# A 16th up-projection pair by seven products in the first MLP, and two moved low parts in the last two

## The reference, cut to what matters

```python
h2 = rms_norm(x, ffn_norm)                       # first MLP
u = causal_dwconv(h2 @ w_up, conv_w, conv_b)
a, bval = jnp.split(u, 2, axis=-1)
x = x + (jax.nn.silu(a) * bval) @ w_down
...
hn = rms_norm_2(h, norm_mix_g[1]); qkv = hn @ w_qkv      # second layer, ahead of its attention
...
h = jax.nn.relu(xn @ w_in); y = (h * h) @ w_out          # last two MLPs
```

## Time and profile before

| | us |
|---|---|
| median of 3 runs | 1708.62 (1707.88 to 1710.52) |
| profiled execution | 1708.18 |
| its span | 1705.8 |
| PE busy | 1693.6 (99%) |
| DVE, ACT, POOL busy | 1135.9, 899.8, 1022.7 |

### The profile page before, as it was taken

The page is one execution under the profiler, slowest core; times in us unless marked ns, Lnnn a source line. Parts: engine busy times, 40 slices in busy tenths (PEclk is TensorE's granted clock), DMA queues, the critical chain, the costliest instruction groups (busy, mean ns, idle before and its releaser), DMA issues.

```text
span 1705.8 us, 28211 instructions
## 1 busy us (share of the span) xinstructions
PE 1693.6 (99%) x9965; PEld 1456.8 (85%) x9965; DVE 1135.9 (67%) x2214; ACT 899.8 (53%) x1635; POOL 1022.7 (60%) x1076
## 2 busy tenths in 40 slices
PE   9999999999999999999999999999999999999998
PEld 7778889999888778888989898977777889898988
DVE  6875788887411455667767666777777675757576
ACT  5665556787422444435454544556565454535355
POOL 6444678787654434457565657755554665666666
PEclk9999999999999999999999999999999999999999
DMA  5221332332223222223323232232321232222222
GB/s 190 78 69 53 109 116 95 116 108 83 92 99 142 96 69 84 73 84 116 109 89 112 87 112 90 94 129 84 117 105 52 87 136 99 99 100 99 100 98 75
DMA packets 48682, 168.17 MB, mean 99 GB/s; under 512 B 5376, under 2 KB 6672, under 8 KB 48528
## 3 DMA queue, kind: packets, MB, share of 16 engines
q1 hardware_dynamic: 48272, 166.05, 28.4%
q10 hardware_dynamic: 288, 0.52, 0.1%
HBM read 164.31 MB, written 2.24 MB: 98 GB/s over the span
## 4 chain that ended last, share of the span: by engine, by line
PE 88%; DVE 5%; POOL 3%; issue 2%; ACT 2%; DMA 1%; SPq 0%; DVEq 0%; ACTq 0%; POOLq 0%
PE bank L928 18%; PE bank L1690 6%; PE bank L1699 6%; PE bank L1691 6%; PE bank L852 6%; PE bank L853 6%; PE bank L858 6%; PE bank L1268 3%; PE bank L1276 3%; PE bank L1269 3%; PE bank L946 3%; PE bank L952 3%; PE bank L947 3%; PE bank L1329 2%; PE bank L1320 2%; PE bank L1322 2%
## 5 line engine op out<-in xcount | busy, mean ns | idle before, releaser
L624 POOL TENSOR_TENSOR w_lo<-stage,w_hi 128x256 fp32r<-128x256 f32 x664 | 527.2, 826 | 423.4 <-ACT w_hi L1752 220.7
L1752 ACT ACTIVATE w_hi<-stage 128x1024 fp32r<-128x1024 f32 x166 | 174.7, 1053 | 165.8 <-PE bank L928 51.8
L853 PE MATMUL bank<-xn_lo,w_hi 128*128 128x512 f32 x544 | 211.8, 389 | 0.0
L852 PE MATMUL bank<-xn_hi,w_hi 128*128 128x512 f32 x544 | 211.8, 389 | 0.0
L928 PE MATMUL bank<-xn_hi,w_hi 128*128 128x512 f32 x464 | 189.0, 407 | 0.0
L928 PE MATMUL bank<-xn_lo,w_hi 128*128 128x512 f32 x464 | 181.8, 392 | 0.0
L3424 DVE TENSOR_TENSOR x<-x,bank 128x256 f32<-128x256 f32 (+1 forms) x217 | 97.5, 455 | 89.2 <-PE bank L1699 86.5
L1699 PE MATMUL bank<-arena 128*128 128x256 f32 x896 | 146.6, 283 | 0.0
L858 PE MATMUL bank<-xn_hi,w_lo 128*128 128x512 f32 x544 | 135.0, 389 | 0.0
L1690 PE MATMUL bank<-arena 128*128 128x256 f32 x512 | 129.4, 284 | 1.2 <-DVE arena L3444 0.6
L1691 PE MATMUL bank<-arena 128*128 128x256 f32 x512 | 128.7, 283 | 0.0
(11 more groups left out here) (506 smaller groups left out, 4305.1 us busy)
## 6 DMA issues: line engine op xcount, KB each, us to landing
stage<-weights SPq DMA_DIRECT2D x189, 512.0 KB, 3.2
stage<-pairs SPq DMA_DIRECT2D x46, 512.0 KB, 3.3
prob<-pairs SPq DMA_DIRECT2D x32, 512.0 KB, 3.2
bias<-table SPq DMA_DIRECT2D x11, 896.0 KB, 5.4
xn_raw<-pairs SPq DMA_DIRECT2D x14, 512.0 KB, 4.2
out<-y SPq DMA_DIRECT2D x8, 256.0 KB, 2.2
x<-x_in SPq DMA_DIRECT2D x3, 512.0 KB, 7.4
bias<-swa_table SPq DMA_DIRECT2D x4, 256.0 KB, 3.5
```

The source lines that it names most:

```text
L624: ins = nc.gpsimd.tensor_tensor(w_lo[:, p_, ks], stage[:, p_, ks], w_hi[:, p_, ks].bitcast(F32), ALU.subtract)
L852: pe.matmul(G[p_][:], w_hi[:, p_, k], hi[:, k], start=(first and k == ks[0]), stop=False)
L853: mm = pe.matmul(G[p_][:], w_hi[:, p_, k], lo[:, k], start=False, stop=False)
L1752: act.activation(w_hi[:, p_], stage[:, p_], ACT.Copy).then_inc(hi_ready, 1)
```

## The change

The edits:

1. N_PLAIN 7 to 6, so Q_UP 16, N_UP1 12. FACTORS_AT stays, so factor quad 3 is made during the last pair but one. The 16th quad lies in `stage`; SP's wait ahead of the down tiles is for quad 15's A22 low part.
2. POOL's list: since 3 is now N_PLAIN - 3, the low parts of factor quads 2 and 3 both come behind the split of the last plain tile.
3. POOL makes T1's low part of factor quad 3 alone, then A11's low part of quad 0, then the low parts of T3, T2 and T4.
4. S1 of quad 0 waits for the first of these, S2 of quad 0 (and ACT's S4 high) for the last.
5. `tile(..., inside=4)`: the norm's two matmuls come after three of the eight weight blocks of tile 1.
6. In the last factor quad of each round of the last two MLPs, ACT and DVE make T2's high and low part first, DVE ahead of adding product S1, then T3's and T4's together.
7. The count of `factor_low` that S2's last block waits for goes with it.

```diff
-N_PLAIN = 7
+N_PLAIN = 6
...
+X_LOWS = QUADS + 1
...
+        outer_sums = flat_tmp[:, 5 * HS:8 * HS].rearrange("p (c s) -> p c s", c=3)[:, 0:3:2]
...
                 pool.wait_ge(ffh_ready, 2 * k + 2)
                 ks = slice(k * HS, (k + 1) * HS)
-                nc.gpsimd.tensor_tensor(factor[:, F_T1:, 1, ks], factor_parts[k % 2][:, 2 * S:].rearrange("p (c s) -> p c s", c=4),
-                                        factor[:, F_T1:, 0, ks].bitcast(F32), ALU.subtract).then_inc(factor_low, 1)
+                e = factor_parts[k % 2]
+                if k < QUADS - 1:
+                    nc.gpsimd.tensor_tensor(factor[:, F_T1:, 1, ks], e[:, 2 * S:].rearrange("p (c s) -> p c s", c=4),
+                                            factor[:, F_T1:, 0, ks].bitcast(F32), ALU.subtract).then_inc(factor_low, 1)
+                    return
+                nc.gpsimd.tensor_tensor(factor[:, F_T1, 1, ks], e[:, 2 * S:2 * S + HS], factor[:, F_T1, 0, ks].bitcast(F32),
+                                        ALU.subtract).then_inc(factor_low, 1)
+                if N_PLAIN - 2 in FACTORS_AT:
+                    up_low(HI_A11, 0)
+                nc.gpsimd.tensor_tensor(factor[:, F_T3:, 1, ks], e[:, 2 * S + HS:].rearrange("p (c s) -> p c s", c=3),
+                                        factor[:, F_T3:, 0, ks].bitcast(F32), ALU.subtract).then_inc(factor_low, 1)
...
-            for k in (HI_A11, HI_A12, HI_S4):
+            for k in (HI_A12, HI_S4) if N_PLAIN - 2 in FACTORS_AT else (HI_A11, HI_A12, HI_S4):
...
+                if inside is not None:
+                    highs(ks[:3], True)
+                    norm(inside)
+                    highs(ks[3:], False).then_inc(hi_free, 1)
+                    pe.wait_ge(lo_ready, 2 * m + p_ + 1)
+                    lows(ks, True).then_inc(tile_done, 1)
...
                 elif k == HI_S2:
                     pe.wait_ge(up_moved, moved_at(q, P1_COPY))
+                    if q == 0:
+                        pe.wait_ge(factor_low, X_LOWS)
...
-                norm(4)
-                tile(T // 2, 1, xn_hi, xn_lo)
+                tile(T // 2, 1, xn_hi, xn_lo, inside=4)
...
-                    if j == 0:
+                    if j == 0 and i == QUADS - 1 and f == F_T2:
+                        pe.wait_ge(factor_low, X_LOWS + N_CH * l + n + 1)
+                    elif j == 0:
...
-            act.wait_ge(factor_low, QUADS)
+            act.wait_ge(factor_low, X_LOWS)
...
+                            if i == QUADS - 1:
+                                act.wait_ge(u_ready, fc_at(l, n, i) + 3)
+                                act.activation(fc_hi[:, i, F_T2], flat_tmp[:, 6 * HS:7 * HS], ACT.Copy).then_inc(factor_made, 1)
+                                act.wait_ge(u_ready, fc_at(l, n, i) + 4)
+                                act.activation(fc_hi[:, i, F_T3:F_T4 + 1:2], outer_sums, ACT.Copy).then_inc(ffh_ready, 1)
...
                         if e == KD - 1:
+                            dve.wait_ge(factor_made, QUADS + N_CH * l + n + 1)
+                            dve.tensor_tensor(fc_lo[:, i, F_T2], flat_tmp[:, 6 * HS:7 * HS], fc_hi[:, i, F_T2].bitcast(F32),
+                                              ALU.subtract).then_inc(factor_low, 1)
                             add_product(q, HI_S1)
...
+                            dve.wait_ge(ffh_ready, FFH_BEFORE + u + 4)
+                            dve.tensor_tensor(fc_lo[:, i, F_T3:F_T4 + 1:2], outer_sums, fc_hi[:, i, F_T3:F_T4 + 1:2].bitcast(F32),
+                                              ALU.subtract).then_inc(ff_ready, 1)
```

More of the change, by code:

```diff
@@ L833, in _, with tile @@
             skip = [0]
-            def tile(m, p_, hi, lo, nk=KD, ready=None, late=None):
+            def tile(m, p_, hi, lo, nk=KD, ready=None, late=None, inside=None):
                 pe.wait_ge(hi_ready, 2 * m + p_ + 1)
@@ L859, in lows @@
                     return mm
-                if ready is None and late is None:
+                if inside is not None:
[4 more added lines that the diff above has]
+                    lows(ks, True).then_inc(tile_done, 1)
+                elif ready is None and late is None:
                     highs(ks, True).then_inc(hi_free, 1)
@@ L2457, in mlp2 @@
                                            ACT.Copy).then_inc(ffh_ready, 1)
-                            act.wait_ge(u_ready, fc_at(l, n, i) + 4)
-                            act.activation(fc_hi[:, i, F_T3:F_T4 + 1].rearrange("p c s -> p (c s)"), flat_tmp[:, 5 * HS:8 * HS],
-                                           ACT.Copy).then_inc(ffh_ready, 1)
+                            if i == QUADS - 1:
[3 more added lines that the diff above has]
+                                act.activation(fc_hi[:, i, F_T3:F_T4 + 1:2], outer_sums, ACT.Copy).then_inc(ffh_ready, 1)
+                            else:
+                                act.wait_ge(u_ready, fc_at(l, n, i) + 4)
+                                act.activation(fc_hi[:, i, F_T3:F_T4 + 1].rearrange("p c s -> p (c s)"), flat_tmp[:, 5 * HS:8 * HS],
+                                               ACT.Copy).then_inc(ffh_ready, 1)
                         if e == 2:
@@ L3472, in fast @@
                         if e == KD - 1:
+                            dve.wait_ge(factor_made, QUADS + N_CH * l + n + 1)
+                            dve.tensor_tensor(fc_lo[:, i, F_T2], flat_tmp[:, 6 * HS:7 * HS], fc_hi[:, i, F_T2].bitcast(F32),
+                                              ALU.subtract).then_inc(factor_low, 1)
                             add_product(q, HI_S1)
-                        dve.wait_ge(ffh_ready, FFH_BEFORE + u + 4)
-                        f_low(i, F_T3, F_T4, flat_tmp[:, 5 * HS:8 * HS])
+                            dve.wait_ge(ffh_ready, FFH_BEFORE + u + 4)
+                            dve.tensor_tensor(fc_lo[:, i, F_T3:F_T4 + 1:2], outer_sums, fc_hi[:, i, F_T3:F_T4 + 1:2].bitcast(F32),
+                                              ALU.subtract).then_inc(ff_ready, 1)
+                        else:
+                            dve.wait_ge(ffh_ready, FFH_BEFORE + u + 4)
+                            f_low(i, F_T3, F_T4, flat_tmp[:, 5 * HS:8 * HS])
                     if e == 2:
```

## The result

The changed kernel took 1712.06 us in the median of 19 runs (1710.43 to 1713.70), before 1708.40 in 19 (1707.20 to 1710.52) beside it: 3.66 us more, a ratio of 1.0023 with a 95% interval of 1.0016 to 1.0029. That is just past what I had called no change (3.4 us), with the interval reaching to both sides of it, 1.4 us above the forecast and inside its range. The profiled execution took 1712.21 us, its span is 1710.4 (before: 1708.18 and 1705.8).

The account below looks back on a forecast made before the run. PE, busy 99% of the 1705.8 us span, was taken as the bound. Terms 5.0 - 0.2 + 0.65 + 0.7 - 3.06 - 1.0 = +2.1 on 1708.18 gave 1710.3, with 0.44 for the median 1710.7; range 1705.0 to 1713.4.

Parts of the forecast that it names:

- The chain that sets quad 0: First MLP, quad 0: S2 and S4 wait for ACT's copies behind DVE's fixed order; +5.0 us, bounds +3.3 and +5.6.
- Contention: First MLP's factors: POOL's 1024-column operation no longer holds DVE's first difference but holds T4's; -0.2 us.
- Rounds: Last two MLPs, eight rounds: PE's stop before S2's last block goes; -3.06 us, bounds 0 and -3.1.
- Norm: Norm's sums: six matmuls cover PE's wait for the low part of the squares' sum; -1.0 us.
- T1 first: Quad 0's S1: T1's low part, made alone and first by POOL, is done about 264.8, hidden by S1's own wait.
- The clock, rival 1: Quad 0's waits before S2 and S4: grant falls from 2.4 to 1.2 GHz, about 2.5 us lost, 1713.2; chance 0.15.
- a granted clock under 1.00: PE at 268 to 277 us: named as a sign that the forecast is wrong.
- a wait of 1.1 at quad 1's S4: PE in quad 1: a wait of about 1.1 us at S4, named as a sign that the forecast is right.
- The last quad: Quad 15 and first down tiles: down loads wait for POOL's A22 low part; +0.7 us, bounds 0 and 1.3.
- P5's copy still beats S4: Last quad: P5's copy ends 5.5 us into it, ahead of S4 at 5.76, despite ACT's first down split at 4.2.
- Quad 2's load: Quad 1: the low part ending at 277.5, which releases this load, is 0.75 behind quad 0's S4; +0.65 us.
- the sibling's part: Edits 5 to 7, in the last two MLPs and the norm: -3.06 and -1.0 us, -4.06 in the forecast.

Follow-up runs that it names:

- x6: Changed kernel with POOL's last factor operation whole again, 1024 columns ahead of A11's low part, instead of T1's low part first; 1712.49 us, ratio 1.0024 to before.
- x3: Changed kernel plus 15 products of 512 columns that nothing reads, in PE's gap before quad 0's S2; 1710.58 us, ratio 1.0015 to before.
- x2_first_mlp_only: Changed kernel with only six plain pairs and T1 first kept, the last two MLPs and the norm as before; 1715.84 us, ratio 1.0046 to before.
- x11: Changed kernel with quad 2's load waiting for the last plain tile alone, no longer for quad 0's A22 low part; 1710.85 us, ratio 1.0012 to before.
- x10: Changed kernel with 15 unread products in PE's gap and the two homes of the raw quads exchanged; 1708.07 us, ratio 0.9997 to before.
- x7: Changed kernel with DVE working in the order quad 0 needs and ACT making P1's and P5's copies earlier; 1712.74 us, ratio 1.0023 to before.
- x9: Changed kernel with DVE and ACT reordered for quad 0 and the homes of the raw quads exchanged; 1707.50 us, ratio 0.9994 to before.
- x5: Changed kernel with raw quads' homes exchanged: odd in the spare blocks, even from 2 on in the stage; 1709.33 us, ratio 1.0003 to before.
- x4: Changed kernel with tile (5,1)'s scaling ahead of two convolutions on DVE, P1's copy ahead of quad 1's on ACT; 1710.48 us, ratio 1.0016 to before.
- x1: Kernel before with only T2 made and waited for by itself and the norm inside the tile; 1703.67 us, ratio 0.9974 to before.

## Why the prediction was right, and where it was not

**Right.** The chain that sets quad 0: factors, DVE's fixed order, conv_0, P1's and P5's copies. S2 was due at 274.3 and came at 273.96, S4 at 276.7 and came at 276.35; the term measured +4.63 beside 4.8 in the profiles. Contention: POOL's operation did move from the T2 side to T4, which took 2.50 us under it. The Trainium skill's rule of the port (SBUF — State Buffer, Who interferes with whom) held in this row as in before's: 2.50 us for 0.84. Rounds: -2.90 for -3.06. Norm: -1.01 for -1.0; alone, the two gave -4.33. T1 first, which I had hidden behind S1's wait, is indeed worth nothing by medians, but for another reason: what it saves is spent in S2's wait (`x6`).

**The clock, rival 1, came true.** I gave it 0.15, and the last sentence of the prediction had named a granted clock under 1.00 here as a sign of being wrong. One of its signs of being right, a wait of 1.1 at quad 1's S4, is missing in the changed kernel: PE at half clock came too late to wait, and with the clock kept the wait is there (`x3`). My argument against it was that PE is dense up to the gap, and that was worth nothing: in the changed kernel's profile the grant fell all the same, 1.5 us behind the gap. I had the price as 2.5; it was 1.92 in a pair of profiles and 1.0 to 1.3 by medians, since a slow PE hides quad 1's wait. The Trainium skill (TensorE: Matmul & The Clock Gate, HAM oscillation) warns of such gaps, and this trace agrees: PE stood 3.7 us and the grant went to 0.50.

**The last quad was mis-sized.** I had +0.7, bounds 0 and 1.3. The profile of the changed kernel has about 1.5 (0.30 at S4, the rest in the down tile), the table of medians 1.5 to 1.8. The step that failed is "P5's copy still beats S4". I had SP's issue 0.8 us into the quad, the first load's landing 3.5 behind it and P5's copy over at 5.5, ahead of S4's 5.76. In the changed kernel's profile the landing was as I had it (issue 425.57, ACT's split 429.06), but the quad began at 424.48, so the issue came 1.1 and the split 4.6 into it, and P5's copy was over at 5.9. The landing itself was not safe either: in `x2_first_mlp_only` ACT started 5.2 us behind the issue (424.77 and 430.00), and PE waited 2.03 us at S4; in `x6` and `x11` the landing took 5.1 and PE waited 1.9. In before these loads were issued 9 us ahead of that quad (408.61), and none of that could be seen.

**Quad 2's load** measured 0.66 between the two profiles with the clock kept (10.85 and 10.19), for 0.65; by medians 1.1 to 1.3. Slower landings than the profiled one may be why (ACT could take quad 2's block 4.5 to 5.7 us after its issue in the profiles in which it waited for it); no run separates that.

In the measure of medians the miss of 1.6 (+3.66 for +2.1) is 1.1 of clock, 1.0 of the last quad and 0.5 of the load, less 0.3 that the sibling's part gave more, and less 0.7 by which the start of quad 0 cost less (`x10`, -0.20 against -4.33, is 4.1, where I had 4.8). Each of these is smaller than one comparison's interval, and they are an account, not a measurement. Three terms of the first MLP were too low by 2.6 together and two others stood 1.0 against them: that the time still fell inside the forecast's own range, 1708.8 to 1712.4, owes something to luck, and without the two it would have lain above it. No term had the wrong sign.

## What to carry to other kernels

Before making an engine faster at one place, look for the floor under the next: a load whose issue hangs on the same chain, and a copy of it that stands in order on an engine whose other work is urgent. `x7` brought quad 0's S4 2.7 us forward in its profile, with the clock kept there, and gained nothing until the load's floor was gone (`x9`). When a loop's count changes parity, follow what sits in which buffer at both ends; exchanging the homes gave 2.9 us here by medians, where the products in place of the plain pair saved PE 0.80. And price a load that comes onto the path by its slow landings, not by the one in the profile.

## What was not expected of the hardware

- Where the granted clock falls is not fixed against the gap: 1.5 us after its end in the changed kernel's profile, within it in those of `x2` and `x5` (0.79 and 0.61 over 272 to 274 us). Half speed lasted 6.8 us in the profiles of the changed kernel, `x2` and `x5`, and 3.4 us in those of `x4` and `x11`, nothing between. What decides it stays open. By the mean clock it did not fall at all in 4 executions of 27 with the same gap.
- A shorter gap is not safe: in the profile of `x4` the clock fell with no gap over 2.6 us, in that of `x6`, with gaps of 2.3 and 2.7, it did not. By the mean clock it fell in most other executions of `x6` and `x7`; a reading of 0.998 alone is weak, since 3 executions of before and 1 of `x1` show it without such a gap.
- Fifteen products that nobody reads, put into the gap, keep the clock at 1.00 in the profile and its mean at 0.999 in all 11 executions of `x3`, and save about 1 us by medians (1.0 to 1.3 in three pairs).
- The first of two 512 KB loads issued back to back from the same queue, by the same line and at the same place (the first down weights), let ACT start 3.3 to 3.7 us after its issue in five profiles (3.5 in the changed kernel's) and 5.1 to 5.2 in three (`x2`, `x6`, `x11`), nothing between.
